# A three-block layer on one core: RMS norm chains tile by tile, last projections by row tiles, one gain vector loaded earlier, and state-space products in turn over the groups of the array

## What is computed

```python
def rms_norm(x, g):
    x32 = x.astype(jnp.float32)
    y = x32 * lax.rsqrt(jnp.mean(x32 * x32, axis=-1, keepdims=True) + NORM_EPS)
    return (y * g.astype(jnp.float32)).astype(x.dtype)
...
def second_block(x, norm_in_g, w_in, ...):
    xn = rms_norm(h, norm_in_g)
    ...
    h = h + jnp.einsum('bte,ed->btd', mixed, w_out)
    return rms_norm(h, norm_out_g)
...
def _s5_mixer(h, w_in, ...):
    # u: 2048 channels in 128 groups of 16; 64 complex states for each group
    bu = lax.complex(jnp.einsum('blgi,gpi->blgp', u32, jnp.real(b_bar)),
                     jnp.einsum('blgi,gpi->blgp', u32, jnp.imag(b_bar)))
    _, states = lax.associative_scan(combine, (a, bu), axis=1)
    y = (jnp.einsum('blgp,gip->blgi', jnp.real(states), c_re.astype(f32))
         - jnp.einsum('blgp,gip->blgi', jnp.imag(states), c_im.astype(f32)))
    ...
    return y.astype(h.dtype) @ w_out
```

## Time and profile before

| what | value |
|---|---|
| device time, median of 3 runs | 2367.45 us (2365.8 to 2368.61) |
| device time of the profiled execution | 2367.97 us |
| its span, first to last instruction | 2366.2 us |
| PE busy | 2170.4 us (92%) |
| DVE busy | 749.6 us (32%) |
| ACT busy | 466.2 us (20%) |
| POOL busy | 65.2 us (3%) |
| mean granted clock of TensorE | 0.969 |

### The profile page before, as it was taken

One profiled execution on the slowest core, in us unless ns is written; L12 is line 12 of the kernel. 1 busy time (PEld: TensorE's weight loads), 2 busy tenths in 40 slices (PEclk: granted clock), 3 DMA queues, 4 the chain that ended last, 5 costly groups with the idle time before them and its releaser, 6 DMA issues.

```text
span 2366.2 us, 29984 instructions
## 1 busy us (share of the span) xinstructions
PE 2170.4 (92%) x11393; PEld 1144.2 (48%) x11394; DVE 749.6 (32%) x1831; ACT 466.2 (20%) x923; POOL 65.2 (3%) x79
## 2 busy tenths in 40 slices
PE   5999987999999998999988996997989997999998
PEld 4844444343333333333333334644464446888873
DVE  1596243222222221222222212342022255777100
ACT  1011111111111111111111101132021107886100
POOL 0000000000000000000000001000000000221000
PEclk8999997999999999999999998999989998999999
DMA  9544566769999999999966997442333241222240
GB/s 347 210 160 178 204 229 248 315 267 419 417 419 417 419 417 384 418 418 418 418 276 271 419 413 253 144 174 108 108 118 142 71 151 72 102 78 72 98 168 37
DMA packets 158855, 591.29 MB, mean 250 GB/s; under 512 B 5323, under 2 KB 6928, under 8 KB 125888
## 3 DMA queue, kind: packets, MB, share of 16 engines
q1 hardware_dynamic: 152512, 573.08, 61.7%
q0 software_dynamic: 4384, 16.40, 1.9%
q10 hardware_dynamic: 1887, 0.81, 0.1%
HBM read 589.23 MB, written 1.05 MB: 249 GB/s over the span
## 4 chain that ended last, share of the span: by engine, by line
PE 75%; DMA 14%; DVE 4%; ACT 3%; DVEq 2%; issue 2%; ACTq 0%; SPq 0%
PE PS L608 25%; PE PS L886 14%; DMA W<-in_w_gu 12%; PE PS L596 9%; PE PS L909 6%; PE PS L1084 4%; PE PS L833 2%; PE PS L922 2%; PE PS L1157 1%; PE PS L665 1%; DVE BIG L1877 1%; PE PS L850 1%; DVE BIG L1881 1%; DMA W<-in_w_mod 1%; PE PS L1145 1%
## 5 line engine op out<-in xcount | busy, mean ns | idle before, releaser
L608 PE MATMUL PS<-W,BIG 128*128 128x512 f32 x1344 | 583.3, 595 | 5.1 <-DVE BIG L2311 2.9
L886 PE MATMUL PS<-W,BIG 128*64 128x512 f32 x2048 | 451.8, 595 | 21.0 <-DMA W<-in_w_gu 20.8
L608 PEld LDWEIGHTS PS<-W,BIG 128*128 128x128 f32 x1344 | 255.8, 191 | 322.9 <-issue 316.4
L886 PEld LDWEIGHTS PS<-W,BIG 128*64 128x64 f32 x2048 | 142.1, 137 | 312.9 <-issue 270.8
L909 PE MATMUL PS<-W,BIG 128*64 128x512 f32 x1024 | 229.1, 600 | 6.9 <-ACT BIG L1363 6.9
L596 PE MATMUL PS<-BIG,W 128*128 128x256 f32 x1024 | 224.0, 381 | 1.4 <-ACT BIG L349 1.4
L596 PEld LDWEIGHTS PS<-BIG,W 128*128 128x128 f32 x1024 | 195.5, 191 | 29.6 <-ACT BIG L349 2.2
L1875 DVE TENSOR_SCALAR BIG<-PS 128x512 f32<-128x512 f32 (+1 forms) x38 | 24.7, 649 | 381.7 <-PE PS L886 355.9
L909 PEld LDWEIGHTS PS<-W,BIG 128*64 128x64 f32 x1024 | 71.1, 138 | 144.1 <-issue 126.4
L1084 PE MATMUL PS<-BIG,W 128*128 128x256 f32 x512 | 118.8, 386 | 0.3 <-ACT BIG L1517 0.3
L1358 ACT ACTIVATE BIG<-BIG 128x512 f32<-128x512 f32 x32 | 20.2, 630 | 488.8 <-DVE BIG L1875 488.8
(11 more groups left out here) (451 smaller groups left out, 1922.0 us busy)
## 6 DMA issues: line engine op xcount, KB each, us to landing
W<-in_w_gu SPq DMA_DIRECT2D x128, 2048.0 KB, 17.6
W<-in_w_dn SPq DMA_DIRECT2D x64, 2048.0 KB, 19.2
W<-in_w_in SPq DMA_DIRECT2D x24, 2048.0 KB, 13.8
W<-in_w_mod SPq DMA_DIRECT2D x12, 2048.0 KB, 9.5
W<-in_gla_w_in SPq DMA_DIRECT2D x10, 2048.0 KB, 7.6
W<-in_s_w_in SPq DMA_DIRECT2D x8, 2048.0 KB, 8.8
W<-in_s_w_glu SPq DMA_DIRECT2D x8, 2048.0 KB, 8.1
W<-in_w_out SPq DMA_DIRECT2D x6, 2048.0 KB, 7.9
```

What stands on the lines that cost most here:

```text
L608: ins = pe.matmul(ps[:, t, :], lhs(i * KT + k)[:, t * P:(t + 1) * P], w[:, k, :], start=i + k == 0, stop=last_chunk and k == KT - 1)
L886: ins = pe.matmul(PS[hh[h], g, :], XET[:, k, :], gu_w(k)[:, g * D + h * CH:g * D + (h + 1) * CH], start=False, stop=k == KT - 1, skip_grou ...
```

## The change

It has four parts.

1. `rms_scale` and `act_rms` work tile by tile: a square, a drain and a root for tile 0, then for tile 1; a reciprocal, a drain and a scaling for tile 0, then for tile 1. What follows is told of each tile. In front of the norms behind go and so ACT takes one more root of eight numbers, whose result is not used.
2. The second unit of w2o, go and so runs by `dense_by_rows`: tile 0 over both chunks, then tile 1 over both. A new semaphore, `first_rows`, tells DVE that tile 0 is done. The number of products is the same.
3. norm_in_g_2 leaves the ring of vectors: POOL loads it into TAB2 behind `mod_done`, before the experts begin. Since the tables that POOL loads into TAB2 would overwrite it, three of them now wait for the norm's rows, and two others go ahead of them.
4. In `from_state` the loop over q is inside, so that four products in a row go to four different quarters of the array's columns; in `drive` the loop over q2 is inside, so that two products in a row go to different halves of its rows.

```diff
+FIRST_ROWS = {"w2o": 1, "go": 2, "so": 3}
...
-           ("post2_g", 0, D), ("post2_b", 0, D), ("norm_in_g_2", 0, D), ("norm_out_g_2", 0, D),
+           ("post2_g", 0, D), ("post2_b", 0, D), ("norm_out_g_2", 0, D),
...
-        def rms_scale(dve, dst, src, gain):
+        def rms_scale(dve, dst, src, gain, done):
 
-            root_taken(dve)
-            return [dve.scalar_tensor_tensor(dst[:, t, :], src[:, t, :], RS[:, t:t + 1], gain, ALU.mult, ALU.mult)
-                    for t in range(TT)]
+            for t in range(TT):
+                norms_out[0] += 1
+                dve.wait_ge(std_ready, norms_out[0])
+                dve.reciprocal(RS[:, t:t + 1], SD[:, t:t + 1])
+                dve.drain()
+                done(dve.scalar_tensor_tensor(dst[:, t, :], src[:, t, :], RS[:, t:t + 1], gain, ALU.mult, ALU.mult))
+            dve.drain()
...
                 act.activation(unused[:, t, :], src[:, t, :], ACT.Square, accum_out=VE[:, t:t + 1])
-            act.drain()
-            act.activation(SD[:], VE[:], ACT.Sqrt, scale=1.0 / D, bias=RMS_EPS).then_inc(std_ready, 1)
+                act.drain()
+                act.activation(SD[:, t:t + 1], VE[:, t:t + 1], ACT.Sqrt, scale=1.0 / D, bias=RMS_EPS).then_inc(std_ready, 1)
...
+                    pool.wait_ge(ev("mod_done"), len(MODS))
+                    pool.dma_start(TAB2[:], A["norm_in_g_2"].unsqueeze(0).to_broadcast([P, D])).then_inc(ev("gain_landed"), 16)
-                if name == "norm_in_g_2":
+                if name == "post2_b":
                     pool.wait_ge(ev("block1_done"), 1)
...
+            def dense_by_rows(name, lhs):
+
+                u, _, chunks, c0 = UNIT[name]
+                ps = unit_ps(name)
+                pe.wait_ge(unit_free[u % 2], u // 2)
+                for t in range(TT):
+                    for i in range(2):
+                        if t == 0:
+                            pe.wait_ge(w_landed[slot_no(c0 + i)], load_count(c0 + i))
+                        w = slot(c0 + i)
+                        for k in range(KT):
+                            ins = pe.matmul(ps[:, t, :], lhs(i * KT + k)[:, t * P:(t + 1) * P], w[:, k, :],
+                                            start=i + k == 0, stop=i == 1 and k == KT - 1)
+                        if t == 1:
+                            ins.then_inc(chunk_done, 1)
+                    if t == 0:
+                        ins.then_inc(ev("first_rows"), 1)
...
                 for h in range(2):
-                    for q2 in range(2):
-                        r = slice(64 * q2, 64 * q2 + 64)
-                        for a in range(2):
+                    for a in range(2):
+                        for q2 in range(2):
+                            r = slice(64 * q2, 64 * q2 + 64)
                             ins = pe.matmul(PS[:, 2 * b + q2, (2 * h + a) * S5_N:(2 * h + a + 1) * S5_N], BTW[b][r, 2 * h + a, :],
...
-                for q in range(PAIRS):
-                    o = PS[32 * q:32 * q + 32, 6 + b]
-                    for a, x_ in enumerate((PA[b], SA[b])):
-                        pe.matmul(o[:, S5_N:2 * S5_N], CTW[b][:, a, q].rearrange("p b i -> p (b i)"), x_[:, q, :],
-                                  start=False, stop=a == 1, skip_group_check=True)
-                        ins = pe.matmul(o[:, 1:S5_N], CTW[b][:, 2 + a, q].rearrange("p b i -> p (b i)"), x_[:, q, 0:S5_N - 1],
-                                        start=False, stop=a == 1, skip_group_check=True)
+                for a, x_ in enumerate((PA[b], SA[b])):
+                    for q in range(PAIRS):
+                        pe.matmul(PS[32 * q:32 * q + 32, 6 + b, S5_N:2 * S5_N], CTW[b][:, a, q].rearrange("p b i -> p (b i)"),
+                                  x_[:, q, :], start=False, stop=a == 1, skip_group_check=True)
+                    for q in range(PAIRS):
+                        ins = pe.matmul(PS[32 * q:32 * q + 32, 6 + b, 1:S5_N], CTW[b][:, 2 + a, q].rearrange("p b i -> p (b i)"),
+                                        x_[:, q, 0:S5_N - 1], start=False, stop=a == 1, skip_group_check=True)
...
             act.activation(work[5], TH, ACT.Sin, scale=TWO_PI / 2).then_inc(ev("s5_setup"), 1)
+            act.activation(HSD[:, 0:8], HVE[:, 0:8], ACT.Sqrt)
             act_rms(act, X, row(1))
...
                 for i in range(2):
-                    wait_unit(dve, f"{name}{i}")
+                    if i == 0:
+                        wait_unit(dve, f"{name}0")
                     for t in range(TT):
+                        if i == 1 and t == 0:
+                            dve.wait_ge(ev("first_rows"), FIRST_ROWS[name])
+                        elif i == 1:
+                            wait_unit(dve, f"{name}1")
                         xs = X[:, t, i * CH:(i + 1) * CH]
```

More of the change, by code:

```diff
@@ L548, in _ @@
                         pool.dma_start(GW2[:, a], A[w].rearrange("n i o -> i n o")).then_inc(ev("gate_w_landed"), 16)
+                    pool.dma_start(WGR, A["gla_w_in_3"][0][:, 5 * D:5 * D + GLA_R].rearrange("(k p) r -> p k r", p=P)) \
+                        .then_inc(ev("tables_landed"), 16)
+                    pool.dma_start(MASK, A["k_causal"]).then_inc(ev("tables_landed"), 16)
+                    pool.wait_ge(ev("rows_ready"), NORMED["xn"] + TT)
                     pool.dma_start(ROT, A["k_rot"].rearrange("(t p) c -> p t c", p=P)).then_inc(ev("tables_landed"), 16)
@@ L551, in _ @@
                     pool.dma_start(WGU, A["gla_w_gate_up_3"][0]).then_inc(ev("tables_landed"), 16)
-                    pool.dma_start(WGR, A["gla_w_in_3"][0][:, 5 * D:5 * D + GLA_R].rearrange("(k p) r -> p k r", p=P)) \
-                        .then_inc(ev("tables_landed"), 16)
-                    pool.dma_start(MASK, A["k_causal"]).then_inc(ev("tables_landed"), 16)
                 if name == "norm_out_g_2":
@@ L993, in _ @@
             pe.wait_ge(ev("yl_ready"), 1)
-            for i in range(2):
-                dense(f"w2o{i}", lambda k: YRT[:, k, :] if k < KT else R2[:, k - KT, :])
+            y2 = lambda k: YRT[:, k, :] if k < KT else R2[:, k - KT, :]
+            dense("w2o0", y2)
+            dense_by_rows("w2o1", y2)
             for t in range(TT):
@@ L1063, in _ @@
             columns_ready("og")
-            for i in range(2):
-                dense(f"go{i}", lambda k: OGT[:, k, :])
+            dense("go0", lambda k: OGT[:, k, :])
+            dense_by_rows("go1", lambda k: OGT[:, k, :])
             for t in range(TT):
@@ L1199, in _ @@
             pe.wait_ge(ev("glu_ready"), 4)
-            for i in range(2):
-                dense(f"so{i}", lambda k: G16[:, k, :])
+            dense("so0", lambda k: G16[:, k, :])
+            dense_by_rows("so1", lambda k: G16[:, k, :])
         @block.scalar
@@ L1426, in _ @@
             copy_columns(act, "yr", YRT)
-            act_rms(act, X, row(9))
+            act_rms(act, X, row(8))
             act_rms(act, X, row(8))
@@ L1944, in _, with row_done @@
             dve.sem_inc(ev("block1_done"), 1)
-            for ins in rms_scale(dve, row(2), X, vector(dve, "norm_in_g_2")):
+            def row_done(ins):
                 ins.then_inc(ev("rows_ready"), 1)
-            dve.drain()
-            dve.sem_inc(v_used, 1)
+            dve.wait_ge(ev("gain_landed"), 16)
+            rms_scale(dve, row(2), X, TAB2[:], row_done)
             dve.wait_ge(ev("lam_ln"), 1)
@@ L2066, in _ @@
             add_to_x("w2o")
-            for ins in rms_scale(dve, X, X, vector(dve, "norm_out_g_2")):
-                row_in(ins)
-            dve.drain()
+            rms_scale(dve, X, X, vector(dve, "norm_out_g_2"), row_in)
             dve.sem_inc(v_used, 1)
-            for ins in rms_scale(dve, row(9), X, vector(dve, "gla_norm_3")):
-                ins.then_inc(ev("rows_ready"), 1)
-            dve.drain()
+            rms_scale(dve, row(9), X, vector(dve, "gla_norm_3"), row_done)
             dve.sem_inc(v_used, 1)
@@ L2246, in _ @@
             add_to_x("go")
-            for ins in rms_scale(dve, row(9), X, vector(dve, "s5_norm_3")):
-                ins.then_inc(ev("rows_ready"), 1)
-            dve.drain()
+            rms_scale(dve, row(9), X, vector(dve, "s5_norm_3"), row_done)
             dve.sem_inc(v_used, 1)
@@ L2312, in _ @@
             add_to_x("so")
-            for ins in rms_scale(dve, X, X, vector(dve, "final_norm_3")):
-                ins.then_inc(ev("result_ready"), 1)
+            rms_scale(dve, X, X, vector(dve, "final_norm_3"), lambda ins: ins.then_inc(ev("result_ready"), 1))
 INPUTS = ["x", "c", "w_mod", "b_mod", "w_in", "b_in", "conv_w", "conv_b", "ln_a_g", "ln_a_b", "w_a", "b_a",
```

## The result

The changed kernel takes 2329.28 us (median of 4 runs, 2325.68 to 2335.16), the kernel before in the same set 2367.26 (2365.80 to 2368.61). The ratio is 0.984, 95% interval 0.982 to 0.987: 38 us less. I had forecast 2331.5 and a range of 2326 to 2343. A second set gave 2326.68 (5 runs) and a ratio of 0.983 (0.982 to 0.985). The profiled run took 2326.36 us with a span of 2324.5, 41.7 less than the 2366.2 of the earlier trace rows.

A forecast was written before the change was run, and what follows sets the result against it. PE was taken as the bound, busy 2170.4 of 2366.2 us. Terms 4.0 + 3.7 + 3.9 + 3.4 + 21.0 = 36.0 us gave a span of 2330.2 and a median of 2331.5 us, range 2326 to 2343.

The forecast's parts named there:

- Start of block 2: Block 2's first norm: with the gain loaded early and tiles in turn, the projection starts 4.0 us earlier.
- Behind w2o: Norms after projection w2o: PE goes on 9.95 us behind its last product instead of 13.68, saving 3.7 us.
- Behind go: Norm after projection go: turned columns ready at 6.4 to 6.8 us instead of 10.65, table load hidden; 3.9 us.
- Behind so: Kernel's end: last scaling ends 3.84 us behind PE's last product instead of 7.30, saving 3.4 us.
- The loop: State-space loop: pass falls from 12.86 to 11.39 us, PE staying the bound; 21.0 us together, bounds 1 to 26.
- The modulation rows: Block 1 products of the same shape, 64 records in 1.95 us over four quarters; they priced `from_state` at 1.01 us.
- loads and products alternate: Rival in `from_state`: each load waits for the product ahead, 4.8 us more a pass; about 2420 us, chance 0.03.
- No other engine became the bound: Rival in the loop: DVE or ACT sets the pass, 2332 to 2340; chance 0.12, shared with quarters overlapping in part.
- The gain vector cost the experts nothing: Moving the gain's transfer ahead of the experts was costed at nothing, or 1.3 us without the expert weights' lead.
- The clock, a rival at 2326 to 2330: Clock may stay up behind go or w2o, products 1 to 3 us shorter each; inside the 0.75 for 2326 to 2337.
- The sum of 36.0: Four norm places and the loop: 4.0 + 3.7 + 3.9 + 3.4 + 21.0 us off the profiled span.
- the likeliest case: Whole kernel: the forecast with its small terms and the clock's luck either way, 2326 to 2337 us, chance 0.75.

The follow-up runs named there:

- late_gain: The changed kernel with the gain of block 2's first norm loaded in its old turn, when its buffer comes free; one run, 2334.41 us.
- no_table: The changed kernel without the two extra roots that make ACT load its table early; one run, 2334.12 us.

## Why the prediction was right

- **Start of block 2, 4.0 us forecast, 3.6 measured.** The mechanism is as put. What the term missed: DVE's reciprocal starts 0.5 us behind the end of ACT's root (1442.92 against 1442.40), where elsewhere it is 0.04 to 0.1. Why stays open; it is the same in both traces. The tile-by-tile norm, which I counted into this term, is worth nothing without the early load (`late_gain`) and beside it about 0.7 us by the estimate above.
- **Behind w2o, 3.7 forecast, 3.9 measured**, 3.5 where the clock went the longer way.
- **Behind go, 3.9 forecast.** ACT's next stage starts 4.8 us earlier behind P; where the clock went the longer way the first turned matrix comes 4.1 us earlier (7.62 behind P, not 11.71). The whole piece gained 6.6 in the changed kernel's trace, since the clock did not fall there. The load of the table is gone as said, but the credit was wrong: the row order does it alone.
- **Behind so, 3.4 forecast, 3.5 measured.**
- **The loop, 21.0 forecast, 20.9 measured, the last part by luck.** The pass came out at 11.39 us as worked out, `from_state` at 1.01 and `drive` at 1.09. The modulation rows were the right row to price from. Counted from one `from_state` to the next, the first pass gained 1.7 us (1.2 forecast), and twelve passes at full pace, not eleven, gained 17.7. The pass behind them, where PE waits for ACT up to the GELU, gained 0.5 (I had 0.85 for the last pass with a fill), and the last two `from_state` 2.7. That makes 22.6. Against it went 1.7 us that my sum did not have: the clock fell ahead of so, where before it had not.
- **The rivals.** That loads and products alternate fell: four loads start 7 ns apart, and 32 records with a load each take 1.01 us. The Trainium skill (TensorE: Matmul & The Clock Gate, The mechanism) lets a weight load overlap with products only when the row groups differ; here all use all rows, and the measurement decides against that as a general rule. The same page of the Trainium skill (Why this matters for your kernels) has outputs in different column groups run side by side, and with that the trace agrees: products to the four quarters start 7 ns apart. No other engine became the bound: DVE had 0.9 us a pass to spare and ACT 0.5. The gain vector cost the experts nothing: it landed at 366.7, and PE's first expert began at 389.8 (389.9 before).
- **The clock, a rival at 2326 to 2330, is what decided the last microseconds.** The sum of 36.0 was made with the clock falling as before. On the longer way the change gains 34.7 us from the experts' end (936.8 - 902.1), on the shorter one 41.0, and the forecast of 2331.5 lies between the two groups of runs. The places of the rival were right, and its sizes (1 to 3 us each) nearly: between the two ways 2.9 us lie behind w2o (1.7 of them go again to a short fall at 1885), 3.6 behind go and 1.4 from there to P of so. What I did not see is that both can come for the same instructions, so that the likeliest case has two values and no run lies at its middle; six of nine runs are below 2327. And the fall was not 10 to 14 us long at each border, as I wrote: at the start of block 2 the kernel before had the lower clock for 20.5 us.

## What to carry to other kernels

Where small products fill a part of the array's columns, issue them so that neighbours go to different quarters: a quarter takes 0.109 us a record for its own load, and four of them share that time. A chain between engines is shortened most by what lets its first half start under the last products (2.6 of the 3.4 us behind so), and a table load or a root then needs no care of its own; look at what the path holds after the edit before crediting an edit. And cost an idle stretch of PE twice, once as idle and once by the clock behind it: here 126 unneeded products in six gaps gave 8 us, more than any single norm chain.

## What was not expected of the hardware

- The same PE program with the same idle time took two ways: with the first turned rows 5.66 us behind P of w2o in all, the lower clock lasted 3.4 us in three traces and 10.2 in three others, and behind go it did not fall in the first three and fell for 10.2 us in the others. Between the changed kernel and `no_table` that was 6.2 us in sum.
- A gap of 2.9 us ahead of so was enough for the clock to fall in the changed kernel (1.7 us lost), while the gap of the same length in the kernel before went without a fall.
- Groups of products in different quarters follow each other at half their length: 1.01, 1.46 and 2.38 us for one, two and four groups.
- Extra products of 128 columns cost 0.23 us each at full clock (56 records, 28 products, in 6.5 us) and held up nothing where they ended ahead of the wait behind them; in the last expert, where they came late, they cost 1 us.
